# Gated linear attention in a two-block forward pass: from four chunk steps to two tiles of 128 tokens

## What is computed

```
def gla_chunked(q, k, v, gk):
    """S_t = diag(a_t) S_{t-1} + k_t v_t^T ; o_t = S_t^T q_t.
    q,k,gk (B,H,N,C,dk) with gk = log a_t, v (B,H,N,C,dv)."""
    incl = idx[:, None] >= idx[None, :]
    bc = jnp.cumsum(gk, axis=-2)
    b_ref = bc[..., CHUNK // 2:CHUNK // 2 + 1, :]
    a_qk = jnp.einsum('bhnid,bhnjd->bhnij', q * jnp.exp(bc - b_ref), k * jnp.exp(b_ref - bc))
    o_intra = jnp.einsum('bhnij,bhnje->bhnie', jnp.where(incl, a_qk, 0.0), v)
    q_dec = q * jnp.exp(bc)
    k_dec = k * jnp.exp(bc[..., -1:, :] - bc)
    g_end = jnp.exp(bc[..., -1, :])
    def step(state, inp):
        q_c, oi_c, k_c, v_c, ge = inp
        o = jnp.einsum('bhcd,bhde->bhce', q_c, state) + oi_c
        state = ge[..., :, None] * state + jnp.einsum('bhcd,bhce->bhde', k_c, v_c)
        return state, o
```

## Time and profile before

| | |
|---|---|
| median of three runs | 1309.19 us |
| the profiled execution | 1308.15 us |
| its span, first to last instruction | 1306.9 us |
| TensorE busy | 1293.2 us, 99% |
| VectorE busy | 819.8 us, 63% |
| ScalarE busy | 690.4 us, 53% |
| GpSimd busy | 112.3 us, 9% |
| DMA, read | 216.14 MB, 168 GB/s over the span |

### The profile page before, as it was taken

The page is one execution under the profiler, slowest core; times in us unless marked ns, Lnnn a source line. Parts: engine busy times, 40 slices in busy tenths (PEclk is TensorE's granted clock), DMA queues, the critical chain, the costliest instruction groups (busy, mean ns, idle before and its releaser), DMA issues.

```text
span 1306.9 us, 16199 instructions
## 1 busy us (share of the span) xinstructions
PE 1293.2 (99%) x6470; PEld 1072.5 (82%) x6470; DVE 819.8 (63%) x1106; ACT 690.4 (53%) x1022; POOL 112.3 (9%) x105
## 2 busy tenths in 40 slices
PE   8999999999999999999999999999999999999998
PEld 6888888888878888888888888998768888888886
DVE  5647755556886665555578877748656565654453
ACT  6664544444866544444376655347544455544443
POOL 0210000000310010000002120010210000100101
PEclk9999999999999999999999999999999999999999
DMA  8755566754645657665545432333328453556561
GB/s 287 225 158 161 173 218 207 235 186 148 206 149 169 209 161 237 186 189 186 171 138 178 145 113 83 97 97 103 92 96 299 144 186 100 192 192 199 172 199 59
DMA packets 119277, 220.36 MB, mean 169 GB/s; under 512 B 8305, under 2 KB 54129, under 8 KB 119201
## 3 DMA queue, kind: packets, MB, share of 16 engines
q1 hardware_dynamic: 115312, 206.08, 49.3%
q0 software_dynamic: 2736, 10.46, 2.4%
q10 hardware_dynamic: 1152, 2.78, 0.6%
HBM read 216.14 MB, written 3.15 MB: 168 GB/s over the span
## 4 chain that ended last, share of the span: by engine, by line
PE 96%; DVE 1%; ACT 1%; DMA 1%; issue 0%; SPq 0%; ACTq 0%; DVEq 0%
PE ps L340 27%; PE ps L342 26%; PE ps L341 26%; PE ps L705 2%; PE ps L717 2%; PE ps L357 1%; PE ps L728 1%; PE ps L562 1%; PE ps L869 1%; PE ps L907 1%; PE ps L681 1%; PE ps L919 1%; PE ps L510 1%; PE ps L692 1%; PE ps L867 1%; PE ps L892 1%
## 5 line engine op out<-in xcount | busy, mean ns | idle before, releaser
L1367 DVE TENSOR_TENSOR spl<-raw,spl 128x1024 fp32r<-128x1024 f32 x387 | 467.9, 1231 | 153.9 <-ACT spl L940 153.0
L940 ACT CAST spl<-raw 128x1024 fp32r<-128x1024 f32 x387 | 399.8, 1050 | 195.7 <-PE ps L342 105.8
L340 PE MATMUL ps<-spl,xs 128*128 128x512 f32 x1056 | 421.5, 399 | 0.0
L342 PE MATMUL ps<-spl,xs 128*128 128x512 f32 x1056 | 412.0, 390 | 0.0
L341 PE MATMUL ps<-spl,xs 128*128 128x512 f32 x1056 | 411.3, 389 | 0.0
L342 PEld LDWEIGHTS ps<-spl,xs 128*128 128x128 f32 x1056 | 198.2, 188 | 42.5
L340 PEld LDWEIGHTS ps<-spl,xs 128*128 128x128 f32 x1056 | 198.5, 188 | 41.5 <-issue 2.7
L341 PEld LDWEIGHTS ps<-spl,xs 128*128 128x128 f32 x1056 | 198.6, 188 | 38.6 <-issue 0.2
L340 PE MATMUL ps<-spl,ys 128*128 128x512 f32 x496 | 200.5, 404 | 0.1
L342 PE MATMUL ps<-spl,ys 128*128 128x512 f32 x496 | 194.2, 391 | 0.0
L341 PE MATMUL ps<-spl,ys 128*128 128x512 f32 x496 | 193.5, 390 | 0.0
(11 more groups left out here) (298 smaller groups left out, 1125.2 us busy)
## 6 DMA issues: line engine op xcount, KB each, us to landing
raw<-in_w_in SPq DMA_DIRECT2D x112, 512.0 KB, 3.7
raw<-in_w_gate_up SPq DMA_DIRECT2D x176, 256.0 KB, 4.1
raw<-in_mlp_w SPq DMA_DIRECT2D x64, 512.0 KB, 4.3
raw<-in_w_down SPq DMA_DIRECT2D x44, 512.0 KB, 4.4
raw<-in_w_out SPq DMA_DIRECT2D x24, 512.0 KB, 3.6
raw<-in_xattn_wk SPq DMA_DIRECT2D x8, 512.0 KB, 4.0
raw<-in_xattn_wv SPq DMA_DIRECT2D x8, 512.0 KB, 3.6
raw<-in_w_branch_gdn SPq DMA_DIRECT2D x8, 512.0 KB, 3.6
```

The costliest lines, as they stand in the source:

```text
L340: self.do.matmul(bank, xh, hi, start=start, stop=False)
L342: m = self.do.matmul(bank, xl, hi, start=False, stop=stop)
L940: self.do.copy(self.k.spl[:, u % NH, 0, :], self.k.raw[:, u % NR, :]).then_inc(*self.up("hi", (u,)))
L1367: self.do.tensor_tensor(lo, self.k.raw[:, u % NR, :], hi.bitcast(F32), ALU.subtract).then_inc(*self.up("lo", (u,)))
```

## The change

The four chunk steps become work on whole tiles of 128 tokens.

- The corner of a tile's scores between its second chunk's queries and its first chunk's keys is filled in: `gla_cross`, eight products with 64 weight columns and 64 moving columns on TensorE, two copies into `lat` on ScalarE.
- GpSimd then multiplies the first chunk's keys by the second chunk's decay, and the last chunk's queries by the third chunk's decay, each 128x256 elements, so that both are taken to the border between the tiles.
- Only tile 0's keys are transposed (four transposes), and only one state is formed, that of tile 0, by four products (`gla_state`). ScalarE evacuates it. The VectorE additions and GpSimd's decay of the state go.
- `gla_read(t)` makes a tile's output: four products of scores and values, and for tile 1 four more of queries and state, each for 128 tokens at once.
- `gla(E)` has 14 pieces, at steps 47, 48, 48, 49, 50, 51, 53, 54, 55, 56, 57, 59, 61, 63: cross scores at 57, transposes at 59, state and tile 0 at 61, tile 1 at 63. The GLA norm of tile 0 moves to 62, 63 and 65.

```
+    def gla_cross(self):                                  # TensorE
+        e4, q = self.s("le4"), self.s("lz")
+        b = self.hold("lc")
+        self.wait_ge(*self.at("dm", "k4"))
+        self.wait_ge(*self.at("pm", "q3"))
+        for t in range(2):
+            for h in range(4):
+                c = h * 256 + t * P
+                m = self.do.matmul(b[0:64, (4 * t + h) * 64:(4 * t + h + 1) * 64], e4[:, c:c + 64], q[:, c + 64:c + P],
+                                   start=True, stop=True)
+        m.then_inc(*self.up("mx", ("lc",)))
     def gla_kturn(self):
         e4 = self.s("le4")
-        for t in range(2):
-            b = self.hold("lk", t)
-            self.wait_ge(*self.at("dm", "k4"))
-            for h in range(4):
-                m = self.do.transpose(b[:, h * P:(h + 1) * P], e4[:, h * 256 + t * P:h * 256 + (t + 1) * P], self.ident())
+        b = self.hold("lk")
+        self.wait_ge(*self.at("pm", "lk"))
+        for h in range(4):
+            m = self.do.transpose(b[:, h * P:(h + 1) * P], e4[:, h * 256:h * 256 + P], self.ident())
-    def gla_step(self, c):
...
+    def gla_state(self):
+        kd = self.s("lkd")
+        for hp in range(2):
+            b = self.hold("ls", hp)
+            self.wait_ge(*self.at("am", "lk"))
+            self.wait_ge(*self.at("ev", f"l{2 + hp}", 0))
+            for i in range(2):
+                h = 2 * hp + i
+                m = self.do.matmul(b[:, i * 256:(i + 1) * 256], kd[:, h * P:(h + 1) * P], self.gla_values(h, 0),
+                                   start=True, stop=True)
+    def gla_read(self, t):
+        at, q, S = self.s2("lat"), self.s("lz"), self.s("lS")
+        for hp in range(2):
+            b = self.hold("lo", t, hp)
+            self.wait_ge(*self.at("am", "lc"))
+            self.wait_ge(*self.at("ev", f"l{2 + hp}", t))
+            if t:
+                self.wait_ge(*self.at("pm", "lq"))
+                self.wait_ge(*self.at("am", "ls", hp))
+            for i in range(2):
+                h = 2 * hp + i
+                o = b[:, i * 256:(i + 1) * 256]
+                if t:
+                    self.do.matmul(o, q[:, h * 256 + P:(h + 1) * 256], S[:, h * 256:(h + 1) * 256], start=True, stop=False)
+                m = self.do.matmul(o, at[:, t, h * P:(h + 1) * P], self.gla_values(h, t), start=(t == 0), stop=True)
...
+    def gla_cross(self):                                  # ScalarE
+        v = self.ps("lc")[0:64, :].rearrange("p (t h n) -> p t h n", t=2, h=4)
+        self.wait_ge(*self.at("mx", "lc"))
+        for t in range(2):
+            self.wait_ge(*self.at("pm", "la", t))
+            a = self.do.copy(h4(self.s2("lat")[0:64, t, :])[:, :, 64:P], v[:, t])
...
+    def gla_cross(self):                                  # GpSimd
+        g = self.small("gend", 16).rearrange("p (h c) -> p h c", c=4)
+        k, q = (h4(self.s(n)) for n in ("le4", "lz"))
+        self.wait_ge(*self.at("mx", "lc"))
+        self.do.tensor_tensor(k[:, :, 0:64], k[:, :, 0:64], bc(g[:, :, 1], 64), ALU.mult).then_inc(*self.up("pm", ("lk",)))
+        self.do.tensor_tensor(q[:, :, 192:256], q[:, :, 192:256], bc(g[:, :, 2], 64), ALU.mult).then_inc(*self.up("pm", ("lq",)))
```

More of the change, by code:

```diff
@@ L827, in gla_gram @@
             self.let(("la", t), "am", "la", t)
+    def gla_cross(self):
[9 more added lines that the diff above has]
+        m.then_inc(*self.up("mx", ("lc",)))
+        self.let(("lc",), "am", "lc")
@@ L829, in gla_kturn @@
     def gla_kturn(self):
         e4 = self.s("le4")
-        for t in range(2):
-            b = self.hold("lk", t)
-            self.wait_ge(*self.at("dm", "k4"))
-            for h in range(4):
-                m = self.do.transpose(b[:, h * P:(h + 1) * P], e4[:, h * 256 + t * P:h * 256 + (t + 1) * P], self.ident())
-            m.then_inc(*self.up("mx", ("lk", t)))
-            self.let(("lk", t), "am", "lk", t)
-    def gla_step(self, c):
[L840 to L844, removed]
-        for hp in range(2):
[L846 to L862, removed]
@@ new lines, in gla_kturn, with gla_values @@
+        b = self.hold("lk")
+        self.wait_ge(*self.at("pm", "lk"))
+        for h in range(4):
+            m = self.do.transpose(b[:, h * P:(h + 1) * P], e4[:, h * 256:h * 256 + P], self.ident())
+        m.then_inc(*self.up("mx", ("lk",)))
+        self.let(("lk",), "am", "lk")
+    def gla_values(self, h, t):
+        return self.s2(f"l{2 + h // 2}")[:, t, (h % 2) * 256:(h % 2 + 1) * 256]
+    def gla_state(self):
+        kd = self.s("lkd")
+        for hp in range(2):
+            b = self.hold("ls", hp)
+            self.wait_ge(*self.at("am", "lk"))
+            self.wait_ge(*self.at("ev", f"l{2 + hp}", 0))
@@ new lines, in gla_state @@
+            m.then_inc(*self.up("mx", ("ls", hp)))
+            self.let(("ls", hp), "am", "ls", hp)
+    def gla_read(self, t):
[13 more added lines that the diff above has]
+                m = self.do.matmul(o, at[:, t, h * P:(h + 1) * P], self.gla_values(h, t), start=(t == 0), stop=True)
+            m.then_inc(*self.up("mx", ("lo", t, hp)))
+            self.let(("lo", t, hp), "am", "lo", t, hp)
@@ L1288, in gla_gram, with gla_state, gla_read @@
             self.do.copy(self.s2("lat")[:, t, :], self.ps("la", t)).then_inc(*self.up("am", ("la", t)))
-    def gla_kturn(self):
[L1291 to L1297, removed]
-        for hp in range(2):
-            self.wait_ge(*self.at("mx", "lo", c, hp))
+    def gla_cross(self):
[4 more added lines that the diff above has]
+            a = self.do.copy(h4(self.s2("lat")[0:64, t, :])[:, :, 64:P], v[:, t])
+        a.then_inc(*self.up("am", ("lc",)))
+    def gla_kturn(self):
+        self.wait_ge(*self.at("mx", "lk"))
+        self.fresh("lkd")
+        self.do.copy(self.s("lkd")[:, 0:512], self.ps("lk")).then_inc(*self.up("am", ("lk",)))
+    def gla_state(self):
+        for hp in range(2):
+            self.wait_ge(*self.at("mx", "ls", hp))
+            self.fresh("lS")
+            self.do.copy(self.s("lS")[:, hp * 512:(hp + 1) * 512], self.ps("ls", hp)).then_inc(*self.up("am", ("ls", hp)))
+    def gla_read(self, t):
+        for hp in range(2):
+            self.wait_ge(*self.at("mx", "lo", t, hp))
             self.fresh(f"lo{t}")
-            self.do.copy(self.s(f"lo{t}")[r, hp * 512:(hp + 1) * 512],
-                         self.ps("lo", c, hp)[r, :]).then_inc(*self.up("am", ("lo", c, hp)))
+            self.do.copy(self.s(f"lo{t}")[:, hp * 512:(hp + 1) * 512],
+                         self.ps("lo", t, hp)).then_inc(*self.up("am", ("lo", t, hp)))
     def xa_turn(self, w, i, src, ready):
@@ L1797, in gla_kdec @@
         self.do.tensor_tensor(e4, e4, self.s("lkT"), ALU.mult).then_inc(*self.up("dm", ("k4",)))
[L1799 to L1810, removed]
     def gla_out(self, t):
@@ L2502, in out_gla @@
 def out_gla(E, t):
-    E.group_sq(("lo", t), E.s(f"lo{t}"), 4, 256, ("am", "lo", 2 * t + 1, 1))
+    E.group_sq(("lo", t), E.s(f"lo{t}"), 4, 256, ("am", "lo", t, 1))
     yield
@@ L2548, in gla @@
     yield
+    E.gla_cross()
+    yield
     E.take("lkd")
     E.gla_kturn()
-    E.give("le4", ("mx", "lk", 1))
+    E.give("le4", ("mx", "lk"))
     yield
[L2553 to L2563, removed]
+    E.take_y("lS")
+    E.take("lo0")
+    E.gla_state()
+    E.give("lkd", ("mx", "ls", 1))
+    E.gla_read(0)
+    yield
+    E.take("lo1")
+    E.gla_read(1)
+    for s in ("lz", "lat", "lS", "l2", "l3"):
+        E.give(s, ("mx", "lo", 1, 1))
+    yield
 def order(E):
@@ L2707, in order @@
          (gdn_scan(E, 1), (56, 57, 58, 59, 60)), (out_gdn(E, 1), (61, 62, 63)),
-         (gla(E), (47, 48, 48, 49, 50, 51, 53, 54, 55, 56, 57, 58, 60, 62, 64)),
+         (gla(E), (47, 48, 48, 49, 50, 51, 53, 54, 55, 56, 57, 59, 61, 63)),
          (gates_in(E, 0), (55, 56)), (gates_in(E, 1), (56, 57)), (gates_in(E, 2), (58, 59)), (gates_in(E, 3), (60, 61)),
-         (out_gla(E, 0), (61, 62, 65)), (part(og, 2), (66, 67)), (ya(), (65, 66)))
+         (out_gla(E, 0), (62, 63, 65)), (part(og, 2), (66, 67)), (ya(), (65, 66)))
     E.spread("yb", lambda E, t, j: (E.s(f"lo{t}")[:, j * 512:(j + 1) * 512], [("dm", "lo", t, j)]), "xs", [("mm", "G3", 1)],
```

9 lines of the change are left out of this document (1 added, 8 removed).

## The result

The changed kernel takes 1295.02 us, the median of four runs (1294.26 to 1295.9), against 1309.15 for the kernel before in the same comparison: a ratio of 0.989, 95% interval 0.9875 to 0.9909. Forecast were 1294.8 us and 14.4 saved; measured are 14.1.

The account below looks back on a forecast made before the run. TensorE's own stream was taken as the bound: 23.07 us removed less 8.65 added saves 14.4, so 1308.15 becomes 1293.75, and with 1.04 for the median 1294.8 us. The range was 1293.5 to 1298.2.

Parts of the forecast that it names:

- What bounds it: Whole kernel: TensorE works 1293.2 of 1306.9 us, holds 96% of the last-ending chain and never waits in the changed stretch.
- What is removed: TensorE's stream: old transposes, four chunk steps and 0.80 us of slower first main products go, 23.07 us in all.
- State and reads: TensorE: tile 0's state 1.73 us, reading tile 0 1.73, reading tile 1 3.45, all on the full array.
- Transposes: TensorE: four key transposes in place of eight, half of 0.87 us, taken as 0.44.
- Cross scores: TensorE: eight products with 64 weight and 64 moving columns, 1.30 us, ends 0.80 and 1.80.
- Leaving the narrow form: First main product behind the cross scores: nothing extra, with 0.20 us as the upper end.
- Cover: Between cross scores and transposes: 6.6 us of other TensorE work hides GpSimd's scalings, 0.7 us each; 4.5 from above.
- ScalarE's wait for the mask: Before copying the cross scores: GpSimd's second mask ends at 917.8 us, before those scores exist, so nothing is lost.
- The branch turn: End of the stretch: moves from 967.38 to 953.0 us; its producer moves to about 943, leaving some 10 cover.
- Dear full products: Rival on TensorE's 256-column products: full ones cost twice a corner's 0.47 us, gain 6.3, time 1302.9; chance 0.02.
- a feed problem: Rival in the shortened stretch: crowded VectorE or late GpSimd scalings make TensorE wait 3 to 6 us, 1299.5; chance 0.09.
- The slower one: Rival: GpSimd holds ScalarE's weight casts, TensorE runs dry and its clock falls to 1.2 GHz, 1329 us; chance 0.02.

Follow-up runs that it names:

- full_shape: The kernel before, its forty 256-column products kept in number and place but each on the full array: 1304.27 us, ratio 0.9965.
- grouped: The kernel before with each chunk's eight output products reordered so the array's shape changes half as often: 1307.17 us beside 1309.68.
- cross_first: The changed kernel with the linear attention's piece ahead of the delta rule's in each step: 1294.98 us.
- mask_10more: The changed kernel with each of GpSimd's two masks done eleven times over in place of once: 1304.03 us.
- no_cover: The changed kernel with the four key transposes issued right behind the cross scores, not two steps later: 1295.47 us beside 1294.9.

## Why the prediction was right, step by step

- *What bounds it.* TensorE's stream was the path and stayed it. No wait entered in the stretch: 34.18 us busy of 34.18.
- *What is removed,* 23.07 us by the starts: right, and `full_shape` confirms the 4.96 that was put on shape. The reading of it was off in one place: 0.47 was taken for the price of a corner product, but it is 0.431 and a share of a change of shape (`grouped`). The sum didn't depend on it.
- *State and reads,* 1.73, 1.73 and 3.45: as forecast, to the hundredth, from the cross-attention row. Transposes 0.44: right.
- *Cross scores.* Mis-sized: 1.30 forecast, 1.08 measured, of which the products are 0.94 and entering their shape is 0.14, a term that the prediction had not set. *Leaving the narrow form*: nothing forecast, 0.20 measured. I had taken it from the products with 32 weight columns, which are of the rounded format and don't show it, rather than from the 0.43 that I had found four times. The two misses nearly cancel: 8.65 forecast, 8.63 measured. That is luck in part; both stood within the bounds given.
- *Cover.* GpSimd's scalings took 0.62 each (0.7 forecast), and keys were ready 6.8 us ahead (6.6 forecast). ScalarE's wait for the mask was over when it was asked, as forecast: the masks ended at 918.30. VectorE worked 22.79 us of the 34.18 (24.3 forecast), ScalarE 20.62 (21). One reason for VectorE's may be that its head norm's product took 2.93 us beside GpSimd's decay of the state before, and takes 1.22 now that this decay is gone (the two lines below). The prediction also counted three state additions fewer in one place and six operations in another; by the code it is four additions and two copies, so the six that its sum uses are right.

```profile
926.93 2.93 DVE L1747 TENSOR_TENSOR ar<-ar,sml 128x1024 f32<-128x1024 f32 x1
```

```profile
926.13 1.22 DVE L1772 TENSOR_TENSOR ar<-ar,sml 128x1024 f32<-128x1024 f32 x1
```

- *The branch turn.* Its place was forecast at 953.0 and is 953.43. Its producer ended at 945.87 + 1.23 = 947.1, not at about 943, so the cover is 6.3 and not 10 us. I had moved VectorE's work rigidly with the stream; it waits there 5.35 us for ScalarE's cast at 942.40. In ScalarE's order that cast stands behind the copies of the state and of tile 0, which end at 939.65, and behind two gate activations, each of which waits for main products (they start at 940.46 and 941.82). It cost nothing.
- *The rivals.* Dear full products and a feed problem did not occur, and `full_shape` rules the first out. The slower one needs a hold far longer than this one: with each mask done six times 0.3 us were lost in the stretch, with eleven times 9. The feed rival came true in no part of the stretch, though VectorE was busy 67% of it.

## What to carry to other kernels

Where one engine's stream is the whole path, price an edit by the distances between starts in that stream and look for the nearest form elsewhere in the same trace. With 256 moving columns, products on a part of the array cost here what full ones cost, one issued behind the other, and each change of shape costs time of its own, so a chunk size below the tile pays twice: in number and in changes. A step that goes through another engine and back was free while 6.8 us of other work stood between. Without them it cost 0.8, and after a wait of 6 us a lower clock added half as much again.

## What the runs showed of the hardware that I had not expected

- A change of the shape in use costs TensorE 0.14 us where a shape with 64 weight columns is entered and 0.20 where one with 128 is, at the 2.4 GHz level, and it falls on the next product whatever its number format (`grouped`, `cross_first`, chunk 3). Only after the rounded products with 32 weight columns it did not show; that was not looked into.
- One pass of GpSimd's mask over 128x512 took 1.51 us beside one operation of VectorE and 0.65 beside another. In the chain of `mask_10more`, and on VectorE meanwhile:

```profile
918.81 1.51 POOL ar L1984
...
920.38 0.65 POOL ar L1984
```

```profile
918.17 1.65 DVE L1392 TENSOR_TENSOR spl<-raw,spl 128x1024 fp32r<-128x1024 f32 x1
919.74 1.20 DVE L1452 TENSOR_REDUCE sml<-ar 128x8 f32<-128x1024 f32 x1
```

The slow pass started beside the splitting of weights, which reads two tensors in SBUF, the fast one beside a reduction, which reads one; with VectorE idle a pass took 0.64 too. So it isn't VectorE's being busy as such. VectorE's 2.93 us above, beside GpSimd's decay, read one tensor and a factor from a second. No run here varied the inputs alone, so the cause is not shown.
- After 6 us without work TensorE's granted clock was 0.50, the 1.2 GHz level, from the transposes at 934.28 to about 940.2. What ran in that time took 3.0 us longer, half of the wait once more. After the 0.75 us of `no_cover` it stayed at 1.00.
